# Reordering the loading phase and the first projection of a four-layer trunk kernel on one core

## The reference

```
h = x * rsqrt(mean(x * x, axis=-1) + EPS) * norm_mix[0]
proj = h @ dsa_w_in          # q, k, v (1024 columns each), q_idx (512), k_idx (64), w_idx (8)
k_idx = rms_norm(k_idx, kidx_gain)
score = sum_heads(w_idx * relu(q_idx . k_idx))   # each query keeps its best 64 keys
```

## Time and profile before

| | us |
|---|---|
| three runs | 1438.90, 1440.65, 1441.47 |
| median of the runs | 1440.65 |
| span of the profiled execution, first to last instruction | 1444.4 |

### The profile page before, as it was taken

The page is one execution under the profiler, slowest core; times in us unless marked ns, Lnnn a source line. Parts: engine busy times, 40 slices in busy tenths (PEclk is TensorE's granted clock), DMA queues, the critical chain, the costliest instruction groups (busy, mean ns, idle before and its releaser), DMA issues.

```text
span 1444.4 us, 33032 instructions
## 1 busy us (share of the span) xinstructions
PE 1393.6 (96%) x13721; PEld 1313.8 (91%) x13721; DVE 1013.8 (70%) x1609; ACT 797.8 (55%) x1315; POOL 648.7 (45%) x362
## 2 busy tenths in 40 slices
PE   8999999999999888999999889999999999999998
PEld 8999999989887777999989779999989998999988
DVE  6775887735595555798879975887845675788841
ACT  5576666544651333576663455666645567575642
POOL 4343365551005202385556954365553332365552
PEclk9999999999999997999999999999999999999999
DMA  6542555553443001376555014455554543455553
GB/s 200 184 134 96 167 193 187 168 194 108 144 146 117 4 4 60 117 206 198 181 173 162 17 49 152 139 192 193 177 189 147 176 146 117 147 176 176 192 169 105
DMA packets 208167, 209.59 MB, mean 145 GB/s; under 512 B 7954, under 2 KB 207170, under 8 KB 208034
## 3 DMA queue, kind: packets, MB, share of 16 engines
q1 hardware_dynamic: 207168, 206.21, 44.2%
q0 software_dynamic: 800, 1.46, 0.5%
q10 hardware_dynamic: 66, 0.02, 0.0%
HBM read 206.62 MB, written 1.05 MB: 144 GB/s over the span
## 4 chain that ended last, share of the span: by engine, by line
PE 83%; DVE 10%; ACT 3%; issue 2%; POOL 1%; DMA 0%; ACTq 0%; DVEq 0%; POOLq 0%
PE psum L422 18%; PE psum L424 17%; PE psum L423 17%; PE psum L824 9%; PE psum L605 6%; PE psum L826 4%; DVE x_low L557 2%; DVE work L2836 1%; ACT w_high L397 1%; DVE work L542 1%; PE psum L1769 1%; PE psum L1783 1%; PE psum L1089 1%; DVE work L2192 1%; PE psum L1100 1%
## 5 line engine op out<-in xcount | busy, mean ns | idle before, releaser
L405 POOL TENSOR_TENSOR w_low<-ring,w_high 128x1024 fp32r<-128x1024 f32 (+1 forms) x185 | 459.4, 2485 | 666.3 <-ACT w_high L397 666.2
L397 ACT ACTIVATE w_high<-ring 128x1024 fp32r<-128x1024 f32 (+1 forms) x368 | 376.4, 1037 | 214.0 <-PE psum L424 123.3
L422 PE MATMUL psum<-x_high,w_high 128*128 128x256 f32 x1728 | 491.1, 284 | 2.4 <-DVE w_low L405 1.4
L424 PE MATMUL psum<-x_high,w_low 128*128 128x256 f32 x1728 | 489.0, 283 | 0.0
L423 PE MATMUL psum<-x_low,w_high 128*128 128x256 f32 x1728 | 489.0, 283 | 0.0
L405 DVE TENSOR_TENSOR w_low<-ring,w_high 128x1024 fp32r<-128x1024 f32 x183 | 295.3, 1615 | 169.7 <-ACT w_high L397 168.4
L422 PEld LDWEIGHTS psum<-x_high,w_high 128*128 128x128 f32 x1728 | 331.6, 192 | 4.8 <-issue 2.2
L423 PEld LDWEIGHTS psum<-x_low,w_high 128*128 128x128 f32 x1728 | 331.7, 192 | 0.0
L424 PEld LDWEIGHTS psum<-x_high,w_low 128*128 128x128 f32 x1728 | 331.6, 192 | 0.0
L824 PE MATMUL psum<-inner,w_high 128*128 128x512 f32 x528 | 186.8, 399 | 0.0
L937 DVE SCALAR_TENSOR_TENSOR work<-psum,par,work 128x255 f32<-128x255 f32 (+1 forms) x352 | 144.5, 472 | 46.2 <-ACT work L856 46.0
(11 more groups left out here) (351 smaller groups left out, 2225.5 us busy)
## 6 DMA issues: line engine op xcount, KB each, us to landing
ring<-in_ffn_w_up_dram SPq DMA_DIRECT2D x88, 1024.0 KB, 5.1
ring<-in_ffn_w_down_dram SPq DMA_DIRECT2D x32, 1024.0 KB, 5.0
ring<-in_dsa_w_in_dram SPq DMA_DIRECT2D x28, 1024.0 KB, 5.2
ring<-in_ffn_w_down_dram SPq DMA_DIRECT2D x16, 768.0 KB, 4.3
ring<-in_rwkv_w_rkv_dram SPq DMA_DIRECT2D x12, 1024.0 KB, 4.9
ring<-in_dsa_w_out_dram SPq DMA_DIRECT2D x8, 1024.0 KB, 5.0
ring<-in_s_w_glu_dram SPq DMA_DIRECT2D x8, 1024.0 KB, 5.3
ring<-in_rwkv_w_out_dram SPq DMA_DIRECT2D x4, 1024.0 KB, 5.0
```

Source lines behind the costliest of these rows:

```text
L397: act.activation(high, raw, ACT.Copy).then_inc(sem("w_rounded", b), 1)
L405: eng.tensor_tensor(low, raw, high.bitcast(F32), ALU.subtract).then_inc(sem("w_split", b), 1)
L422: pe.matmul(out_, lhs[0], rhs[0], start=start, stop=False, skip_group_check=True)
L424: return pe.matmul(out_, lhs[1], rhs[0], start=False, stop=stop, skip_group_check=True)
```

## The change

PE turns the first four chunks of x (8 transposes) before the early parameters; the 12 idle turns after the transposes are dropped and the last 12 become 4. i0 is sent in two transfers of 512 KB, one for each block, whose rows are 128 columns (512 bytes) and no longer 256 columns (1024 bytes). PE runs i0 in a new order: chunk by chunk the four matmuls with the weight's high part, over both blocks; after all chunks the 16 matmuls with the weight's low part, block by block. ACT rounds i0 block by block between the early chunks 1 and 2, and no longer ahead of them. DVE takes the reciprocal ahead of its last copy of x, and moves the subtractions for i0 behind early chunks 3 and 7.

```diff
+        def project_first(pe, x, ready):
+            key = plan.tiles[0]
+            out_ = [bank_of(key)[:, b * T:(b + 1) * T] for b in range(2)]
+            for k in range(DC):
+                ready(k)
+                for b in range(2):
+                    if k == 0:
+                        pe.wait_ge(sem("w_rounded", b), 1)
+                    for i in range(2):
+                        pe.matmul(out_[b], w_high[0][:, b, k, :], x[i][:, k, :], start=(k, b, i) == (0, 0, 0), stop=False,
+                                  skip_group_check=True)
+            for b in range(2):
+                pe.wait_ge(sem("w_split", b), 1)
+                for k in range(DC):
+                    mm = pe.matmul(out_[b], w_low[0][:, b, k, :], x[0][:, k, :], start=False, stop=k == DC - 1,
+                                   skip_group_check=True)
+                half_done(key, mm, b == 0)
+            mm.then_inc(sem("bank_full", plan.bank[key][0]), 1)
...
+        def send_first_tile(sp, w):
+            _, slot, _ = plan.tile[plan.tiles[0]]
+            dst = ring[:, slot, :].rearrange("p (k n) -> p k n", n=TILE)
+            for b, landed_ in ((0, sem("first_block")), (1, sem("weights_in", slot))):
+                sp.dma_start(dst[:, :, b * P:(b + 1) * P], rows(w, 3 * D + b * P, cn=P)).then_inc(landed_, 16)
...
         def load_pe(pe):
             pe.wait_ge(sem("constants"), 2)
             idle_turns(pe, 8)
-            turn_early_params(pe)
             pe.wait_ge(sem("x_moved"), 32)
             for c in range(DC):
+                if c == 4:
+                    turn_early_params(pe)
                 for b in range(TT):
...
-            idle_turns(pe, 12)
-            pe.wait_ge(sem("token_inverse"), 1)
+            pe.wait_ge(vector_step.sem, TOKEN_INVERSE)
...
-            idle_turns(pe, 12)
+            idle_turns(pe, 4)
...
         def load_dve(dve):
-            dve.wait_ge(sem("turned"), 1)
-            dve.tensor_copy(par[:, 0:EARLY_ROWS], banks[4][:, 0:EARLY_ROWS]).then_inc(sem("par_ready"), 1)
             for m in range(4):
-                dve.wait_ge(sem("turned"), m + 2)
+                if m == 2:
+                    dve.wait_ge(sem("turned"), 3)
+                    dve.tensor_copy(par[:, 0:EARLY_ROWS], banks[4][:, 0:EARLY_ROWS]).then_inc(sem("par_ready"), 1)
+                if m == 3:
+                    dve.wait_ge(sem("root"), 1)
+                    assert vector_step.mark(dve.reciprocal(token_rstd, token_rstd)) == TOKEN_INVERSE
+                dve.wait_ge(sem("turned"), m + 1 + m // 2)
                 dve.tensor_copy(xT[:, 2 * m:2 * m + 2, :].rearrange("p a b -> p (a b)"),
                                 banks[m][:, :]).then_inc(sem("x_ready"), 1)
-            dve.wait_ge(sem("root"), 1)
-            dve.reciprocal(token_rstd, token_rstd).then_inc(sem("token_inverse"), 1)
-            start_splits(rest_of_weights, dve, 0, 0)
...
-            start_splits(round_weights, act, 0)
             act.wait_ge(sem("par_ready"), 1)
-            for m in range(4):
+            round_early(act, 0, 0)
+            round_first(act, 0)
+            round_first(act, 1)
+            for m in (1, 2, 3):
                 round_early(act, 0, m)
             start_splits(round_weights, act, 1)
 
+        def round_first(act, b):
+            key = plan.tiles[0]
+            _, slot, count = plan.tile[key]
+            if b == 0:
+                act.wait_ge(sem("first_block"), 16)
+            else:
+                act.wait_ge(sem("weights_in", slot), count)
+            raw, high, _ = split_part(key, b, ring[:, slot, :].rearrange("p (k n) -> p k n", n=TILE))
+            act.activation(high, raw, ACT.Copy).then_inc(sem("w_rounded", b), 1)
...
         def start_dve(dve):
-            start_splits(rest_of_weights, dve, 0, 1)
             for m in range(4):
                 split_early(dve, 0, m)
+                if m % 2:
+                    start_splits(rest_of_weights, dve, 0, m // 2)
             start_splits(rest_of_weights, dve, 1, 0)
```

More of the change, by code:

```diff
@@ L710, in send_dsa @@
             for i in range(2):
-                send_plain(sp, (L, "i", i), w, 3 * D + i * TILE)
+                if L == layers[0] and i == 0:
+                    send_first_tile(sp, w)
+                else:
+                    send_plain(sp, (L, "i", i), w, 3 * D + i * TILE)
             c = 3 * D + IDX_HEADS * HALF
@@ L1128, in values @@
                 mm.then_inc(sem("o_full"), 1)
-            project(pe, (L, "i", 0), early_parts[0], lambda c: early_ready(pe, n, c))
+            if L == 0:
+                project_first(pe, early_parts[0], lambda c: early_ready(pe, n, c))
+            else:
+                project(pe, (L, "i", 0), early_parts[0], lambda c: early_ready(pe, n, c))
             if L == 0:
@@ L2965, in trunk @@
         x_tok = slot_view(0, TT, D)
+        TOKEN_INVERSE = 1
         token_sum, token_rstd = work[:, 6, 1352:1354], work[:, 6, 1354:1356]
```

## The result

The changed kernel takes 1449.38 us (median of four runs, 1447.79 to 1452.99) against 1441.06 for the kernel before (four runs); the ratio is 1.0057, 95% interval 1.0041 to 1.0074. It is **slower**, by 8.3 us in the medians. Run twice more, it was slower again, by ratios of 1.0040 (1.0020 to 1.0060) and 1.0052 (1.0034 to 1.0070). One execution of the first repeat took 2238.43 us at a mean clock of 0.556 and is left out of every figure. The forecast, 1442.7 in a range of 1438.9 to 1445.0, is wrong: right in its sign and much too small. Its rival (a) gave 1444.3, also too small.

The account below looks back on a forecast made before the run. PE, with 83% of the chain, runs without a gap from `turn_ki`, so a shift there reaches the end. VectorE's 1.4 us (k0 late) plus 0.6 us (beside GpSimd) on 1440.65 gave 1442.7, range 1438.9 to 1445.0.

Parts of the forecast that it names:

- rival (a): PE's new wait at `turn_ki`: the clock falls to half rate behind it, 1.6 us more, 1444.3 in all; chance 0.20.
- What bounds, and PE's queue: Start up to `turn_ki`: PE ends i0 2.3 us earlier, at 18.6, reaches `turn_ki` at 31.8 and waits there for VectorE.
- k0's sending: SP's queue: k0 goes out only when both blocks of i0 are split, at 17.3 where it was 14.62.
- k0's landing: k0 takes 5.1 us from issue, lands at 22.45, and VectorE starts its low part 1.4 us later.
- The stalls beside GpSimd: VectorE's chain to `turn_ki`: the first wait stays, the second moves from `mu_rest` to L557; 0.6 us more.
- the rows at 913: Earlier trace: after a stall of 1.91 us at 913.25 the granted clock was 0.50 for 2 us, then 0.72.
- the median taken as the base: The kernel before: 1440.65 us, 3.75 us below the profile's span of 1444.4, to which 2.0 us was added.
- (b): i0's transfer: 512-byte rows cost as much as long ones, k0 1.9 us later, +3.3 to +3.9 us, 1444.3; chance 0.06.
- (c): VectorE's chain sheds both losses beside GpSimd and PE's 2.3 us nearly pass: 1438.7; chance 0.14.
- (d): PE's early start is lost at `turn_ki`, k0 lands in under 4 us: within 0.7 us of 1440.65; chance 0.16.

Follow-up runs that it names:

- experiment 3: Kernel before, with one wait added in SyncE's queue so that k0 is sent only when the last early low part is made: 1447.98 us, ratio 1.0038 to before.
- experiment 4: Changed kernel with VectorE's two subtractions for i0 moved ahead of early chunks 2 to 7: 1442.56 us, ratio 0.9997 to the kernel before.
- experiment 1: Changed kernel run again twice without an edit: 1449.09 and 1449.17 us, ratios 1.0040 and 1.0052 to the kernel before.
- experiment 5: Changed kernel with 28 idle turns in PE's wait ahead of `turn_ki`: 1445.45 us, ratio 1.0020 to the kernel before.
- experiment 7: Changed kernel with i0 sent in one transfer of 1024-byte rows again: 1447.15 us, ratio 1.0044 to the kernel before.
- experiment 8: Changed kernel, i0's block 0 subtraction early, block 1's given to GpSimd, `mu_rest` behind the scaled index keys: 1444.08 us, ratio 1.0019 to the kernel before.
- the first of 9: Kernel before with x turned first, changed reciprocal, 4 idle turns ahead of the first product, i0's subtractions ahead of early chunks: 1444.22 us, ratio 1.0022.
- experiment 6: Kernel before with 40 idle turns ahead of `turn_ki`, a delay with PE kept at work: 1444.98 us, ratio 1.0023.

## Why the prediction was wrong, point by point

**What bounds, and PE's queue: right up to the end of i0.** The transposes start at 6.32 (forecast 6.2), the first product at 11.62 (11.5 to 12.1), i0 is done at 18.81 (18.6), 2.1 us earlier and not 2.3. That a gain of PE ahead of `turn_ki` is worth nothing while VectorE is later was right too. But PE did not reach `turn_ki` at 31.8: VectorE's lateness held it already in k0, by 1.12 and 0.76 us, which the forecast had left out. It took nothing from the sum, since `turn_ki` waits for VectorE anyway, but PE came to it from a stretch with gaps (busy 0.12 of the 1 us from 29 to 30).

**k0's sending: right.** The low part of i0 block 1 ended in time for k0 to be sent at 17.22 (forecast 17.35). That this one step, a wait moved in SP's queue by VectorE's new order, is what costs is shown from both sides: experiment 3 puts a late k0 alone into the kernel before and gets a ratio of 1.0038, experiment 4 sends k0 early again in the changed kernel, by VectorE's order alone, and gets 0.9997.

**k0's landing: the term was mis-sized.** The prediction took 5.1 us from the earlier trace rows; it was 6.5 here, and 6.6, 6.9, 6.2 and 6.8 in the four other profiles with this order of VectorE (experiments 1, 5 and 7), but 5.2 and 5.35 in experiments 4 and 3. The trace of the changed kernel has k1 sent behind k0 before k0 is there, but so has experiment 3, and both 3.4 us behind it (20.62 and 21.10). By 22 us the queues had moved as much since 18 us in either, 265 and 254 GB/s, about one tile. It is not the short rows (experiment 7). What it is stays open. VectorE's start at k0's low part came 2.55 us late where 1.4 was forecast.

**The stalls beside GpSimd: right.** The first stayed (1.77 us), the second moved from `mu_rest` (0.17 us now) to the second group of L557, which took 3.44 us where it took 1.41. In all VectorE's chain became 0.5 us longer; the forecast said 0.6. So `turn_ki` is 3.06 us late where the sum had 2.0.

**The clock: this is the step that failed.** The prediction saw it as rival (a), with its place and its price (1.6 us; 1.5 measured by the mark and by experiment 5), and gave it 0.20, on the ground that PE comes from 15 us of full work. That ground did not hold: the rows at 913 showed a fall after a shorter stall, in the changed kernel PE had gaps in k0, and in experiment 3 the clock fell although 18 us of full work stood ahead of the wait. Between 10 and 44 us all seven profiles in which PE waited 2.29 to 3.25 us had the clock at or near 0.50 within the next 4 us (the changed kernel three times, experiments 3, 7, 8 and the first of 9). Shorter waits went either way: 1.57 us was followed by a fall (experiment 1), 1.54 us was not (experiment 4), nor were those of 1.12 to 1.40 us at the start of k0. None with a wait of at most 0.4 us at `turn_ki` had a fall there. Behind `turn_ki` the price, up to the mark, was 1.3 to 2.5 us. The Trainium skill ("TensorE: Matmul & The Clock Gate", Part 1) says that the array goes back to half rate when idle; the runs agree, and the forecast had the page right and weighed it wrong. The sum put this term at nothing; it measured 1.5 us. With (a) and the longer landing the sum is 3.06 + 1.51 = 4.57 us: 1445.2 against the median taken as the base, which lies beyond the upper end of 1445.0.

**What is still missing.** The forecast missed by 6.7 us. The longer landing makes 1.1 of that (3.06 against 2.0), the clock 1.5, the median taken as base 0.4 (1440.65 against 1441.06), and 3.7 are left. The ratios of the three comparisons make 8.2, 5.8 and 7.5 us (each about 2.7 either way), the first part of the profiles 4.4 to 5.1. What lies between is not found in a place: behind the mark the three profiled executions of the changed kernel took 1283.5, 1281.9 and 1280.4 us, those of the kernel before 1286.35, 1280.1 and 1281.9. The mean clock of the 22 executions of the changed kernel in experiment 1 was 0.9910, of the 66 of before beside them 0.9938: that is 0.0028 x 1448 / 0.5 = 8.1 us more at the lower level, of which the stretch behind `turn_ki` makes 3.4 (2 x (0.47 + 0.38) / 0.5). The other 4.7 us at half speed would cost some 2.3 us, near what is missing between the mark and the ratio in the two repeats (1.4 and 2.4): an estimate from these means, which puts the rest into the clock of later stages. Experiment 6 gives no sign that lateness as such brings this. Whether the rest belongs to the change or to chance is not settled, and the range failed for it: it was built from one median of three runs and from one profile, while single executions of the same kernel lie 11 us apart.

**The other rivals.** (b), the short rows, is refuted by experiment 7. (c) needed VectorE's wait for k0 to be under 0.5 us; it was 3.4 in the changed kernel. In experiment 4, where it was 0.17, the mark was 1.4 us early, but not by (c)'s mechanism: both losses beside GpSimd were still there (1.82 and 1.51 us), and the gain came from k0 being rounded 1.4 us sooner. (d) fell with k0's landing.

## What to carry to other kernels

When an engine's work is reordered, look for the transfer whose sending waits on what moved back: here a subtraction 2.6 us later held SP, k0 behind it, then an in-order queue, and 2.1 us gained on the engine with 83% of the chain were worth nothing. Put the clock's fall into the sum for a new wait of TensorE: behind all seven waits of 2.3 to 3.3 us here it came, behind one of 1.6 us too, and full work ahead of the wait did not prevent it. Count idle turns as part of the schedule: where work moves ahead of them and leaves a gap, new ones have to fill it. Where the time hangs on the clock's falls, compare a mark in the trace ahead of them beside the times of many executions; two spans mislead, and the mark alone shows only what lies ahead of it.

## What the runs showed of the hardware

**GpSimd holds VectorE for the length of an instruction.** An early chunk took 2.63 us in place of 0.47 beside a GpSimd subtraction (experiment 8), and the waits of about 1.8 and 1.5 us in the chain ended within 0.3 us of the end of GpSimd's instruction in the profiles of before and of the changed kernel. It goes the other way too: GpSimd's subtraction at 17.30 took 3.90 us with VectorE's subtraction of 17.71 beside it, where others took 2.4 to 2.5. Giving idle GpSimd a subtraction of VectorE's cost VectorE 4.3 us and saved it 1.2. The Trainium skill ("SBUF — State Buffer", "Who interferes with whom") says that a VectorE instruction with two SBUF inputs contends with a GpSimd instruction that reads SBUF, for ports that are locked exclusively; the early chunks agree. `mu_rest` reads one tile only and was held as well (1.64 us in the earlier trace rows, 0.17 in the changed kernel), so two inputs were not the only case here.

**The clock of the start is not in the granted clock.** That column is 1.00 from the first microsecond, while the transposes of x took 0.21 to 0.23 us each and the idle turns, of the same shape, 0.11 to 0.12 later. By these durations PE ran at the lower level at the start; the column does not show it.

**512-byte rows show no cost here.** With them ScalarE began to round i0 at 9.71 to 9.97, in one transfer at 9.98, and the times did not differ beyond their intervals (ratios to before 1.0040 and 1.0052 with, 1.0044 without).
